# A two-block transformer layer on one core: the second mixer's order and head norms, and the second feed-forward's up products

## What is computed

```python
h = rmsnorm(x, ln_attn_pre)
dq, dk, dv, fq, fk, fv, f_logit = split(h @ w_in)       # 512 columns each, 8 logits
cum = cumsum(log_sigmoid(f_logit + b_f))
lam = exp(sum(lam_q1 * lam_k1)) - exp(sum(lam_q2 * lam_k2)) + lambda_init
# "d" heads (4): two softmax maps of 64 channels, their difference, then a norm of each head's output
pd = softmax(dq dk^T / 8 + bias, causal)
od = rmsnorm((pd[0] - lam * pd[1]) @ dv, subln_g) * (1 - lambda_init)
# "f" heads (8, here 4 pairs)
of = softmax(fq fk^T / 8 + cum_q - cum_k, causal) @ fv
x = x + rmsnorm(concat(od, of) @ w_out, ln_attn_post)
u = square(relu(rmsnorm(x, ln_mlp_pre) @ w_up))         # 1024 -> 4096
x = x + rmsnorm(u @ w_down, ln_mlp_post)
```

## Time and profile before

| | |
|---|---|
| median of 3 timed runs | 879.27 us (873.22 to 879.78) |
| the profiled execution, own time | 876.9 us |
| its span, first to last instruction | 875.1 us |
| granted TensorE clock, mean | 0.994 of full speed |
| second mixer, with its start | 566 to 662 us |
| its output projection and the norm after it | 662 to 701 us |
| second feed-forward | 701 to 866 us |

### The profile page before, as it was taken

How to read it: one execution, slowest core, us unless ns; L and a number is a source line. 1 busy time by engine, 2 the same in 40 slices (tenths; PEclk the granted TensorE clock), 3 DMA queues, 4 the chain that set the end, 5 groups by cost and what they waited for, 6 DMA issues and landing times.

```text
span 875.1 us, 15552 instructions
## 1 busy us (share of the span) xinstructions
PE 854.2 (98%) x6234; PEld 794.5 (91%) x6234; DVE 594.1 (68%) x780; ACT 461.2 (53%) x650; POOL 63.3 (7%) x64
## 2 busy tenths in 40 slices
PE   6999999999999999999999999999999999999997
PEld 6999999999988998899999998898887889999995
DVE  4548986537867587697767777876564686656554
ACT  5457772448656344575545556565464553333332
POOL 0025920000000321000000000000000000000000
PEclk9999999999999999999999999999989999999999
DMA  9644452333442456464564556254423365555531
GB/s 344 227 145 145 146 197 94 117 124 135 145 145 97 169 193 212 150 231 172 178 207 163 192 192 204 91 187 146 145 79 138 121 232 201 191 181 180 182 130 48
DMA packets 22167, 143.82 MB, mean 164 GB/s; under 512 B 2928, under 2 KB 3188, under 8 KB 5728
## 3 DMA queue, kind: packets, MB, share of 16 engines
q1 hardware_dynamic: 20304, 138.30, 44.8%
q0 software_dynamic: 1808, 4.73, 1.6%
HBM read 141.96 MB, written 1.84 MB: 164 GB/s over the span
## 4 chain that ended last, share of the span: by engine, by line
PE 91%; ACT 3%; DVE 3%; issue 1%; DMA 1%; SPq 0%; DVEq 0%; ACTq 0%
PE pj L467 18%; PE pj L469 15%; PE pj L470 15%; PE pa L891 7%; PE pa L892 7%; PE pa L893 7%; PE pj L471 2%; PE pj L472 2%; PE pa L506 2%; PE pj L570 1%; ACT w_hi L1154 1%; PE pj L576 1%; PE pj L572 1%; DVE area L1640 1%; PE po L605 1%
## 5 line engine op out<-in xcount | busy, mean ns | idle before, releaser
L1627 DVE TENSOR_TENSOR w_lo<-w_raw,w_hi 128x2048 fp32r<-128x2048 f32 x127 | 294.4, 2320 | 71.0 <-ACT w_hi L1154 70.8
L467 PE MATMUL pj<-a_hi,w_hi 128*128 128x256 f32 x1168 | 333.1, 285 | 0.7 <-issue 0.7
L470 PE MATMUL pj<-a_hi,w_lo 128*128 128x256 f32 x1168 | 330.4, 283 | 0.0
L469 PE MATMUL pj<-a_lo,w_hi 128*128 128x256 f32 x1168 | 330.4, 283 | 0.0
L1154 ACT ACTIVATE w_hi<-w_raw 128x2048 fp32r<-128x2048 f32 x127 | 242.0, 1907 | 56.7 <-PE pa L893 42.4
L467 PEld LDWEIGHTS pj<-a_hi,w_hi 128*128 128x128 f32 x1168 | 223.9, 192 | 4.9 <-issue 3.9
L469 PEld LDWEIGHTS pj<-a_lo,w_hi 128*128 128x128 f32 x1168 | 223.9, 192 | 0.9
L470 PEld LDWEIGHTS pj<-a_hi,w_lo 128*128 128x128 f32 x1168 | 223.9, 192 | 0.0
L891 PE MATMUL pa<-w_hi,a_hi 128*128 128x512 f32 x280 | 109.3, 390 | 1.4 <-issue 1.4
L892 PE MATMUL pa<-w_lo,a_hi 128*128 128x512 f32 x280 | 109.2, 390 | 0.0
L893 PE MATMUL pa<-w_hi,a_lo 128*128 128x512 f32 x280 | 108.9, 389 | 0.0
(11 more groups left out here) (272 smaller groups left out, 1028.8 us busy)
## 6 DMA issues: line engine op xcount, KB each, us to landing
w_raw<-stream SPq DMA_DIRECT2D x127, 1024.0 KB, 4.8
area<-gains POOLq DMA_DIRECT2D x4, 512.0 KB, 4.2
cst<-consts SPq DMA_DIRECT2D x1, 1093.0 KB, 13.6
x_tok<-x_in SPq DMA_DIRECT2D x2, 512.0 KB, 4.8
w_raw<-stream SPq DMA_DIRECT2D x4, 256.0 KB, 7.0
area<-cmpw POOLq DMA_DIRECT2D x1, 1024.0 KB, 5.7
out<-x_tok SPq DMA_DIRECT2D x4, 256.0 KB, 2.0
t_wide<-t_rows POOLq DMA_DIRECT2D x1, 768.0 KB, 11.3
```

Of the source, the lines that this page charges most:

```text
L467: pe.matmul(out_, a[0], a[1], start=first, stop=False)
L469: pe.matmul(out_, wh, al, start=False, stop=False)
L470: return pe.matmul(out_, wl, ah, start=False, stop=last)
L1627: dve.tensor_tensor(w_lo[:, slot, :], w_raw[:, slot, :], w_hi[:, slot, :].bitcast(F32), ALU.subtract)\
```

## The change

Four things are changed, on all engines together.

- `a_hi` and `a_lo` become the two halves of one tensor, so that chunk k has its high and low 256 columns side by side. `pj` becomes three tensors of a bank each.
- In the second mixer the order of pieces on TensorE, ScalarE and VectorE is another: `dv` 0 comes before the gate logits, scores are issued one unit earlier, and splits, exponentials and reads are placed anew. Head pair f3 uses `ps` like the others.
- The norm of the d heads: two products of `ones` with the squares, 512 columns each, into the banks of `fq` 1 and `fk` 1; ScalarE takes Ln and then Exp with scale -0.5; VectorE multiplies `od`, gain and that factor in one instruction. The one-column products, the root, the reciprocal and `dg8` go.
- In the second feed-forward, up units 2 to 15 are `wide_unit`s: the high weights meet both halves in one product of 512 columns, the low weights the high half in one of 256. The two channel blocks have a bank each, alternately (`pj2`, `po`) and (`pj0`, `pj1`). ScalarE copies the low half's sums out, VectorE adds them. The loop's body has six steps and runs twice.

```diff
-        a_hi = sb("a_hi", [P, 24, T], F32R)
-        a_lo = sb("a_lo", [P, 24, T], F32R)
+        a_hl = sb("a_hl", [P, 24, 2, T], F32R)
+        a_hi, a_lo = a_hl[:, :, 0, :], a_hl[:, :, 1, :]
...
+        wide = ((pj[2], po), (pj[0], pj[1]))
+        fs = V(2, 2, T)
...
@@ TensorE, order of the second mixer @@
+            run_unit(("dv", 0))
             d_scores(0)
-            run_unit(("dv", 0))
+            claim(pe, "O", "flog")
+            pe.wait_ge(S("ws_ready"), 2)
+            narrow_products(8)
+            run_unit(("dq", 1))
             narrow_turn("flog_tok", 8)
-            run_unit(("dq", 1))
+            d_scores(1)
             d_turn(0)
-            d_scores(1)
             run_unit(("dk", 1))
             d_apply(0)
+            d_scores(2)
             d_turn(1)
             run_unit(("dv", 1))
             d_apply(1)
-            d_scores(2)
+            d_scores(3)
             run_unit(("fq", 0))
             f_sums()
             d_turn(2)
-            d_scores(3)
             run_unit(("fk", 0))
             d_apply(2)
             d_turn(3)
+            f_scores(0)
             run_unit(("fq", 1))
             d_apply(3)
-            f_scores(0)
+            f_scores(1)
             run_unit(("fk", 1))
             f_turn(0)
-            f_scores(1)
-
-            claim(pe, "O", "odn")
+            await_value(pe, ("fq", 1))
+            await_value(pe, ("fk", 1))
             pe.wait_ge(S("od_sq_ready"), 1)
-            for h in range(4):
-                for tb in range(2):
-                    mm = pe.matmul(po[:, 2 * h + tb:2 * h + tb + 1], odsq[:, h, tb * P:(tb + 1) * P], ones[:, 0:1],
-                                   start=True, stop=True)
-            written(mm, "O")
+            for q in range(2):
+                mm = pe.matmul(pj[od_banks[q]][:, :], ones, odsq[:, 2 * q:2 * q + 2, :], start=True, stop=True)
+            mm.then_inc(S("od_sums"), 1)
+            f_scores(2)
             run_unit(("fv", 0))
             f_turn(1)
-            f_scores(2)
             f_scores(3)
             f_apply(0)
+            pe.wait_ge(S("od_root"), 1)
             run_unit(("fv", 1))
             f_turn(2)
             f_apply(1)
-            claim(pe, "S", "odn")
-            pe.wait_ge(S("dg8_ready"), 1)
-            for q in range(2):
-                mm = pe.matmul(ps[:, q, :], ones, dg8[:, 4 * q:4 * q + 4, :], start=True, stop=True)
-            written(mm, "S")
             f_turn(3)
             f_apply(2)
             f_apply(3)
...
+            def wide_unit(slot, s):
+                for k in range(KC):
+                    both = a_hl[:, k, :, :].rearrange("p a t -> p (a t)")
+                    for nb in range(2):
+                        c = k * 256 + nb * P
+                        bank = wide[s][nb]
+                        pe.matmul(bank[:, 0:2 * T], w_hi[:, slot, c:c + P], both, start=(k == 0), stop=False,
+                                  skip_group_check=True)
+                        mm = pe.matmul(bank[:, 0:T], w_lo[:, slot, c:c + P], a_hi[:, k, :], start=False,
+                                       stop=(k == KC - 1), skip_group_check=True)
+                mm.then_inc(S("unit_done"), 1)
...
+            await_read(pe, "O", "rbc3")
+            ffn2_step(2, 2, 0, first=True)
...
+            with pe.Fori(0, 2) as m:
+                for q in range(4, 10):
+                    ffn2_step(m * 6 + q, q, m * 3 + (q // 2 - 1))
...
@@ ScalarE @@
+            ahead(("dq", 1))
             await_psum(act, "O", "flog_tok")
             read(act.activation(fl, ...), "O")
-            ahead(("dq", 1))
             act.wait_ge(S("flx_ready"), 1)
             ... Abs, Exp ...
+            act.activation(lf_e, lf_e, ACT.Ln, bias=1.0).then_inc(S("lfe_ready"), 1)
             d_turned(0)
-            act.activation(lf_e, lf_e, ACT.Ln, bias=1.0).then_inc(S("lfe_ready"), 1)
             ahead(("dk", 1))
             exps(9, sm2, pr2)
+            ahead(("dv", 1))
             d_turned(1)
+            exps(10, sm2, pr2)
             token_major(("dv", 1), dv[:, :, 256:512])
             d_out(0)
...
-            read(act.activation(ods, po[:, 0:8], ACT.Sqrt, bias=lm[:, 2:3], scale=1.0 / 128), "O")
+            for q in range(2):
+                A.did(act.activation(od_root[:, 2 * q:2 * q + 2, :],
+                                     pj[od_banks[q]][:, :].rearrange("p (a t) -> p a t", a=2), ACT.Ln,
+                                     bias=lm[:, 2:3], scale=1.0 / 128))
+            A.sync()
+            act.activation(od_root, od_root, ACT.Exp, scale=-0.5).then_inc(S("od_root"), 1)
...
+            def low_copy(i, s):
+                act.wait_ge(S("unit_done"), i * 2 + (v0 - 1))
+                for nb in range(2):
+                    act.activation(fs[:, nb, :], wide[s][nb][:, T:2 * T], ACT.Copy).then_inc(S("low_copied"), 1)
...
@@ VectorE @@
+            dve.wait_ge(S("od_root"), 1)
+            stt(odn, od, prm_("subln"), od_root, ALU.mult, ALU.mult).then_inc(S("odn_ready"), 1)
...
+            def wide_out(i, s, uses):
+                dve.wait_ge(S("low_copied"), i * 2 - 2)
+                for nb in range(2):
+                    tt(fs[:, nb, :], wide[s][nb][:, 0:T], fs[:, nb, :], ALU.add).then_inc(S(f"wide_read{s}"), 1)
+                dve.wait_ge(S(f"wide_read{s}"), uses * 2)
+                tt(fx, fs, rbc2, ALU.mult).then_inc(S("fx_scaled"), 1)
+                dve.wait_ge(S("fx_scaled"), i - 1)
+                stt(fu, fx, 0.0, fx, ALU.max, ALU.mult).then_inc(S("fu_ready"), 1)
```

More of the change, by code:

```diff
@@ L240, in program @@
         ptr2 = [V(24, 2, 384), V(27, 2, 384)]
-        od, odsq, dg8, odn = V(50, 4, T), V(0, 4, T), V(4, 8, P), V(0, 4, T)
+        od, odsq, od_root, odn = V(50, 4, T), V(0, 4, T), V(4, 4, T), V(0, 4, T)
         ncum = V(56, T)
@@ L267, in program @@
         lf_e, fl = small(2, 8), small(2, 8)
-        ods = small(8)
         assert _t[0] <= 1024
@@ L1003, in f_scores @@
                 await_read(pe, "O", "fcum")
-                o_ = [(ps if j < 3 else ps3)[:, hb, :] for hb in range(2)]
+                o_ = [ps[:, hb, :] for hb in range(2)]
                 q = [slice(hb * 64, hb * 64 + 64) for hb in range(2)]
@@ L1519, in _ @@
             ahead(("dv", 0))
-            exps(8, sm2, pr2)
             token_major(("dv", 0), dv[:, :, 0:256])
-            await_psum(act, "O", "flog_tok")
-            read(act.activation(fl, po[:, 0:128].rearrange("p (b x) -> p b x", b=2)[:, :, 0:8], ACT.Copy), "O")
-            ahead(("dq", 1))
-            act.wait_ge(S("flx_ready"), 1)
-            A.did(act.activation(lf_e, fl, ACT.Abs))
-            A.sync()
-            A.did(act.activation(lf_e, lf_e, ACT.Exp, scale=-1.0))
-            A.sync()
             def d_out(p):
@@ L1545, in f_out_hi @@
                 act.activation(a_hi[:, 12 + j, :], fo(j), ACT.Copy).then_inc(S("mix2_hi"), 1)
+            exps(8, sm2, pr2)
+            ahead(("dq", 1))
+            await_psum(act, "O", "flog_tok")
+            read(act.activation(fl, po[:, 0:128].rearrange("p (b x) -> p b x", b=2)[:, :, 0:8], ACT.Copy), "O")
+            act.wait_ge(S("flx_ready"), 1)
+            A.did(act.activation(lf_e, fl, ACT.Abs))
+            A.sync()
+            A.did(act.activation(lf_e, lf_e, ACT.Exp, scale=-1.0))
+            A.sync()
+            act.activation(lf_e, lf_e, ACT.Ln, bias=1.0).then_inc(S("lfe_ready"), 1)
             d_turned(0)
-            act.activation(lf_e, lf_e, ACT.Ln, bias=1.0).then_inc(S("lfe_ready"), 1)
             ahead(("dk", 1))
             exps(9, sm2, pr2)
+            ahead(("dv", 1))
             d_turned(1)
+            exps(10, sm2, pr2)
             token_major(("dv", 1), dv[:, :, 256:512])
@@ L1601, in _ @@
                 up2_hi(i, 8 + 2 * i)
+            def low_copy(i, s):
+                act.wait_ge(S("unit_done"), i * 2 + (v0 - 1))
+                for nb in range(2):
+                    act.activation(fs[:, nb, :], wide[s][nb][:, T:2 * T], ACT.Copy).then_inc(S("low_copied"), 1)
             def ffn2_step(i, m, q, first=False):
                 if not first:
-                    split(v0 + 2 * q, m * 2)
-                up2_hi(i, 8 + 2 * q)
-                split(v0 + 1 + 2 * q, m * 2)
+                    split(v0 + 2 * q, m * 4)
+                low_copy(i, q % 2)
+                up2_hi(i, 8 + 2 * (q % 3))
+                split(v0 + 1 + 2 * q, m * 4)
             ffn2_step(2, 0, 2, first=True)
-            with act.Fori(1, UP2 // 3) as m:
-                for q in range(3):
-                    ffn2_step(m * 3 + q, m, q)
-            ffn2_step(UP2 - 1, UP2 // 3, 0)
+            ffn2_step(3, 0, 3)
+            with act.Fori(0, 2) as m:
+                for q in range(4, 10):
+                    ffn2_step(m * 6 + q, m, q)
             warm_root()
@@ L2298, in _ @@
             stt(a_lo[:, 8:12, :], odn, 1.0 - LAMBDA_INIT, a_hi[:, 8:12, :].bitcast(F32), ALU.mult, ALU.subtract)\
                 .then_inc(S("odn_lo"), 1)
-            f_out_lo(2)
```

(24 more changed lines are left out.)

135 lines of the change are left out of this document (48 added, 87 removed).

## The result

The changed kernel takes 869.14 us (median of 11, 868.49 to 872.66); the kernel before, timed beside it, 876.62 (median of 11, 873.22 to 880.02). The ratio is 0.992 (95%: 0.990 to 0.994): 0.8% faster, within the 1% that I had called hard to tell from no change. The forecast was 870.4 us.

A forecast was written before the change was run, and what follows sets the result against it. TensorE, busy 98% of the span, was taken as the bound. Mixer -6.6, new wait +0.3 and merge -2.6 gave -8.9 us: profiled time 876.9 to 868.0, plus 2.4 for the timed median, 870.4 us; range 864 to 877.

The forecast's parts named there:

- The sum of the mixer: Second mixer: all savings and additions together, -6.6 us, with the output projection starting near 655.4 instead of 662.0.
- The shortened start: Start of the second mixer: with `dv` 0 first, TensorE loses 0.4 us where it lost 0.76.
- the new end: Before the output projection: head-output halves done near 648, only two 0.2 us waits for turned copies stay; 1.35 us won.
- the root's time: Norm of the d heads on ScalarE: finished near 638.7, before `fv` 1 writes its bank at 645.2.
- margins of 0.15 us or less: Mixer: closest hand-overs, keys for `f_scores(0)` ready 614.25, wanted 614.4; `fk` 1's for the sums, 631.8 both.
- Turn 1: Mixer, turn of head 1: starts at 592.75 against 592.54, stall moves little; with the start about 0.4 us net gain.
- Clock falls anyway: Rival, chance 0.12: new short pieces after `fk` 1 lower the clock; the 2.05 us come back, 872.5 us.
- The merge: Second feed-forward, up units 2 to 15: merged pairs save 0.19 us a unit, 2.6 us over 14 units.
- The new wait: First wide unit: waits until VectorE has copied the norm row out of `po`, adding 0.3 us.
- The slack of the down units' weights: Second feed-forward: split weights take 8.5 us, wanted 11.0 us later; 2.5 us of slack, costed at nothing.
- the slower rival: Rival, chance 0.05: the wide unit's ScalarE and VectorE chain is later than its slack; 888 us and more.
- One table for Ln and Exp: Rival, chance 0.05: both functions in one loaded table, so a 1.28 us load at head 1 goes; 869.2 us.

The follow-up runs named there:

- `ffn_only`: The kernel before with only the wide up units and the joined activation tensor, old mixer kept: 872.26 us, ratio 0.9951.
- `layout_only`: The kernel before with only `a_hi` and `a_lo` made halves of one tensor: 875.68 us, ratio 0.9996.
- `wide_sorted`: The changed kernel with each wide unit's block doing its 8 products of 512 columns, then its 8 of 256: 868.15 us, one execution.
- `norm_only`: The kernel before with only the new head norm (new sums, Ln and Exp, one multiplication), in the old order of pieces: 876.57 us, ratio 1.0011.
- `one_col`: The changed kernel with eight one-column products of unused result put in after the scores of f2, before `fv` 0: 873.16 us, ratio 0.9959.

## Why the prediction was right, point by point

- **The sum of the mixer** was -6.6 us; measured is 95.45 - 89.02 = 6.4 us. The shortened start, the two waits of 0.2 us at turned copies (0.17 and 0.18), the new end and the root's time (forecast 638.7, measured 638.5) came as worked out. Of the margins of 0.15 us or less one failed by little: the sums waited 0.17 us. Turn 1 was forecast at 592.75 with about 1.2 us of idle time; it came at 592.51 with 1.01.
- **What that sum is made of** was only partly seen. I charged 2.05 us to the clock and 2.8 to the one-column products. `ffn_only` shows these products at 1.8 us when the clock stays up, so the clock's share is 3.0 us, and the old mixer without it is 92.4 us long in `ffn_only` and `layout_only`: the change's own work in the mixer is worth 3.4 us. The step that I missed is that the earlier trace rows is a state of one execution. The forecast held because that execution was like the median one: half of the 75 executions before have a mean clock below 0.995. That was luck. Had the profile shown one of the 19 at full clock, the same working would have given a gain some 3 us smaller.
- **Clock falls anyway** (0.12) did not happen in the profiled execution. Of 53 executions of the six kernels with the new mixer and nothing added to it (single executions left out), 35 are at full clock, 1 is low and 17 lie between; the three such of the changed kernel take 870.5 to 872.7 us. So falls do still happen, and their means don't say where.
- **The merge** was forecast at 2.6 us for 14 units of 5.56 us. The units take 5.64: 0.11 x 14 = 1.5 us. This is the term that I mis-sized, by 1.1 us. The step that failed is the choice of cadences from long streams of one width for a stream that alternates; `wide_sorted` gave the 5.56.
- **The new wait** was forecast at 0.3 us. The first wide unit starts 694.65 - 655.44 = 39.21 us after the projection, where the old up unit started 700.91 - 662.02 = 38.89 us after it: 0.32.
- **The slack of the down units' weights** was forecast at 2.5 us and is 3.2 us in a late step: VectorE starts two splits at 794.90, the first of them for this down unit, which is ready near 797.2, and TensorE asks for it at 800.40. No wide unit waits in the loop (156.00 of 156 us busy), so the slower rival had no ground. VectorE and TensorE of the changed kernel, by their timelines:

```profile
794.90 4.49 DVE L1638 TENSOR_TENSOR w_lo<-w_raw,w_hi 128x2048 fp32r<-128x2048 f32 x2 [1.12 <-ACT w_hi L1152]
...
800.40 0.40 PE L891 MATMUL pa<-w_hi,a_hl 128*128 128x512 f32 x1
```

- **One table for Ln and Exp** (0.05): the trace still loads twice, here at 633.52 and 636.10.
- **The sum**: -6.4 + 0.3 - 1.5 = -7.6, and the spread product ends 0.15 us earlier: 7.8 us, the span's 875.1 - 867.3. The forecast had 8.9.
- **The time of 870.4 us** is closer than its parts. I added 2.4 us for the distance between the profiled execution before (876.9) and the median of three runs (879.27). With eight more runs that median is 876.62, and the changed kernel's is 869.14 beside 869.12 of its profiled execution: the 2.4 us came by chance out of three runs. Without them the forecast is 868.0, 1.1 us below the measured 869.14, which is the merge's error. The two errors partly cancel: that the absolute time came within 1.3 us is luck too.

Two points stay open: what decides whether the clock falls in an execution, since the means are seldom low in `ffn_only` (1 of 12) and often in `layout_only` (7 of 12) with the same old mixer; and why `norm_only`, without the one-column products of this mixer, has no execution at full clock, with its profiled fall in the first mixer (granted clock 0.50 at 202 us), which the edit doesn't touch. That an edit in one stage shifts falls in another is not excluded for any kernel here.

## What to carry to other kernels

A granted clock below 1.00 in a profile is a property of that execution until several executions show it: compare pieces at the same clock, and count the executions at full clock on both sides. Where merged products leave a stream of two widths, sort it by width and price it so: here 0.08 us of a unit's 0.19 were lost by alternating. A longer serial chain on ScalarE, like the Ln and Exp here, paid only with an order in which TensorE had a whole unit to do meanwhile. And a median of three runs of a kernel that scatters by 7 us is no base for an absolute time.

## What the runs showed of the hardware

- Products with few columns are followed by a granted clock of 0.50 (1.2 GHz) in some executions and not in others of the same kernel. Products of 1 column (632 us) and of 16 columns (198 us) stand before the falls in the traces; that they cause them is not shown. One fall costs 1.5 to 3 us by its length: 95.45 against 92.43 us of the same mixer, 2.9 us in the first mixer of `one_col`, and 7.34 against 5.85 in its `fv` 0.
- A product of 512 columns costs 0.227 us among its like and one of 256 0.119 us, each with its own weights; alternating, a pair costs 5.64 / 16 = 0.3525 us, sorted 5.56 / 16 = 0.3475.
- Ln and Exp after each other cost a table load of 1.28 us each, in the gates and in the root (633.52 and 636.10). The Trainium skill ("ScalarE: Activation LUTs", Table sets) says that one set holds both; no run here shows it.
